# Differential attention: scaling the second map and adding it on GpSimd, with the head norm's epsilon scaled to match

## The reference, cut to what matters

```python
a = softmax(s1) - lam * softmax(s2)          # s1, s2: scores with ALiBi bias and chunk mask
o = a @ v                                    # per head, 128 wide
o = rms(o, g_sub) * (1 - lambda_init)        # o / sqrt(mean(o^2) + EPS), EPS = 1e-6
```

## Time before, and its profile

| what | us |
|---|---|
| three runs: median (lowest, highest) | 3034.1 (3030.89, 3037.03) |
| the profiled execution, span from its first to its last instruction | 3033.2 |
| PE busy in the span | 2847.4 (94%) |
| DVE busy | 1369.0 (45%) |
| ACT busy | 967.3 (32%) |
| POOL busy | 494.7 (16%) |
| stage of differential attention, about | 547 to 943 |
| stage of latent attention, about | 943 to 1354 |
| `mix_out`, about | 1354 to 1600 |
| `mlp`, about | 1600 to 3033 |

### The profile page before, as it was taken

One profiled execution on the slowest core, in us unless ns is written; L12 is line 12 of the kernel. 1 busy time (PEld: TensorE's weight loads), 2 busy tenths in 40 slices (PEclk: granted clock), 3 DMA queues, 4 the chain that ended last, 5 costly groups with the idle time before them and its releaser, 6 DMA issues. The chain is left out here.

```text
span 3033.2 us, 35888 instructions
## 1 busy us (share of the span) xinstructions
PE 2847.4 (94%) x12859; PEld 2275.7 (75%) x12859; DVE 1369.0 (45%) x2743; ACT 967.3 (32%) x1561; POOL 494.7 (16%) x321
## 2 busy tenths in 40 slices
PE   6998898699996999989979999999999999999997
PEld 5996686566674777757767888888887888888886
DVE  5113303688892554534434344343436434343444
ACT  5112212467673443435542121211123111111212
POOL 0010001122220212110012111111114111111112
PEclk8999998799997999999999999999999999999999
DMA  5323218933413111114452111111126111111112
GB/s 181 120 102 94 80 49 290 222 77 88 112 42 126 57 56 60 46 49 130 141 180 91 56 42 55 41 51 46 42 97 222 56 42 48 49 41 55 41 49 97
DMA packets 229877, 267.27 MB, mean 88 GB/s; under 512 B 19392, under 2 KB 174416, under 8 KB 227456
## 3 DMA queue, kind: packets, MB, share of 16 engines
q1 hardware_dynamic: 229760, 265.79, 28.8%
HBM read 187.85 MB, written 77.89 MB: 88 GB/s over the span
## 5 line engine op out<-in xcount | busy, mean ns | idle before, releaser
L1890 DVE TENSOR_TENSOR ff_acc<-ff_acc,ff_ps 128x1024 f32<-128x1024 f32 x240 | 292.3, 1218 | 718.5 <-PE ff_ps L1964 718.5
L1947 PE MATMUL ff_ps<-ff_u_hi,ff_w_hi 128*128 128x512 f32 x1024 | 406.4, 397 | 12.5 <-DVE ff_w_lo L1878 12.5
L1947 PE MATMUL ff_ps<-ff_u_lo,ff_w_hi 128*128 128x512 f32 x1024 | 406.1, 397 | 0.0
L1947 PE MATMUL ff_ps<-ff_u_hi,ff_w_lo 128*128 128x512 f32 x1024 | 405.9, 396 | 0.0
L1964 PE MATMUL ff_ps<-ff_w_hi,ff_hid_hi 128*128 128x512 f32 x1024 | 399.3, 390 | 1.6 <-DVE ff_acc L1890 1.5
L1964 PE MATMUL ff_ps<-ff_w_lo,ff_hid_hi 128*128 128x512 f32 x1024 | 399.1, 390 | 0.0
L1964 PE MATMUL ff_ps<-ff_w_hi,ff_hid_lo 128*128 128x512 f32 x1024 | 398.4, 389 | 0.0
L1855 ACT ACTIVATE work<-ff_ps 128x1024 f32<-128x1024 f32 x64 | 65.6, 1025 | 738.5 <-PE ff_ps L1947 738.5
L1819 POOL TENSOR_TENSOR work<-work 128x1024 f32<-128x1024 f32 x64 | 121.2, 1894 | 1081.9 <-ACT work L1855 1081.9
L1364 PE MATMUL da_ps_s<-da_keys,da_qs 128*128 128x420 f32 (+17 forms) x704 | 219.8, 421 | 33.3 <-DMA late_ident<-in_ident 15.7
L1947 PEld LDWEIGHTS ff_ps<-ff_u_hi,ff_w_hi 128*128 128x128 f32 x1024 | 193.0, 188 | 59.3 <-DVE ff_w_lo L1878 12.9
(11 more groups left out here) (179 smaller groups left out, 4859.3 us busy)
## 6 DMA issues: line engine op xcount, KB each, us to landing
ff_w_raw<-in_w_ff SPq DMA_DIRECT2D x64, 512.0 KB, 4.2
work<-in_w_ff SPq DMA_DIRECT2D x64, 512.0 KB, 3.5
ni_xt<-in_x SPq DMA_DIRECT2D x16, 512.0 KB, 4.3
mo_y<-scr_yT SPq DMA_DIRECT2D x16, 512.0 KB, 5.7
work<-in_x SPq DMA_DIRECT2D x16, 512.0 KB, 4.9
scr_h<-mo_h SPq DMA_DIRECT2D x16, 512.0 KB, 3.3
ff_h_in<-scr_h SPq DMA_DIRECT2D x16, 512.0 KB, 4.3
out<-ff_acc SPq DMA_DIRECT2D x16, 512.0 KB, 5.2
```

The lines of the kernel that those rows point to most:

```text
L1890: dve.tensor_tensor(acc[:, t], acc[:, t], ps2[t % 2][:, :], ALU.add).then_inc(part_added, 1)
L1947: m = pe.matmul(ps1[e][:, cols], w[:, e, k], a[:, k, cols], start=k == 0 and i == 0, stop=k == KD - 1 and i == 2)
```

## The change

For the differential attention only:

- The first map stays unnormalised. Its row sums go into a tile `total1` that keeps all 64 of them (4 heads x 16 rows).
- The step `scale` now stands after the second component and the step `end` is gone. In `scale`, DVE makes the reciprocal of the second sum and the ratio (minus lambda) x t1 / t2; then GpSimd scales the second map in place by the ratio and adds it onto the first, in two instructions with a wait between them.
- DVE waits, before it writes a new row into `second`, for GpSimd's addition of the row two before.
- The list of steps changes with this: the planner's cost of `end` is gone, and a group's first turn stands behind the `scale` of its last row.
- At the end of the stage the 64 sums are squared and multiplied by EPS on ACT, transposed on PE, copied on DVE and stored to DRAM; SP waits for the store.
- In `mix_out` each tile loads the scaled epsilons, spread over the 128 partitions, into `y_rstd` (128x512, one more transfer of 256 KB for a tile); DVE adds the mean from PSUM onto them, and Ln works on the sum instead of on PSUM with a constant bias.

```diff
-                        if c == 0:
+                        if c == COMPS - 1:
                             later.append((SCALE_AFTER, ("scale", 0, i)))
-                        if c == COMPS - 1:
-                            later.append((END_AFTER, ("end", 0, i)))
...
-            return META + P * (step[2] + 1) + 250 if step[0] == "end" and da else 0
+            return 0
...
-                                e[0] == "end" and e[2] - NT * e[1] == 4 * g + 3 - NT * back for e in rows_part[at + 1:]):
+                                e[0] == "scale" and e[2] - NT * e[1] == 4 * g + 3 - NT * back for e in rows_part[at + 1:]):
...
+                if da:
+                    sp.wait_ge(total_copied, 1)
+                    sp.dma_start(scr.eps_total, eps_rows[:, :]).then_inc(total_stored, 16)
+                    sp.wait_ge(total_stored, 16)
...
                 def scaled(h, i, u, **at):
-                    hold(pool, inv_ready, NT * h + i + 1)
-                    pool.tensor_scalar(row(i, u), row(i, u), inv[:, i % 2, 0:1], 1.0, ALU.mult,
-                                       ALU.mult).then_inc(first_scaled if da else probs_ready, 1)
+                    if da:
+                        second_row = comp_row(i, 1, u)
+                        hold(pool, ratio_ready, NT * h + i + 1)
+                        pool.tensor_scalar(second_row, second_row, ratio[:, i % 2:i % 2 + 1], 1.0, ALU.mult,
+                                           ALU.mult).then_inc(second_scaled, 1)
+                        hold(pool, second_scaled, NT * h + i + 1)
+                        pool.tensor_tensor(row(i, u), row(i, u), second_row, ALU.add).then_inc(probs_ready, 1)
...
+                    sums = total1[:, ds(NT * h + i, 1)] if da and c == 0 else total[:, i % 2, c:c + 1]
                     act.activation(comp_row(i, c, u), comp_row(i, c, u), ACT.Exp, bias=nmax[:, i % 2, c:c + 1], scale=scale,
-                                   accum_out=total[:, i % 2, c:c + 1]).then_inc(exp_ready, 1)
+                                   accum_out=sums).then_inc(exp_ready, 1)
...
+                if da:
+                    act.wait_ge(ratio_ready, NT * H)
+                    act.activation(total1[:, :], total1[:, :], ACT.Square, scale=math.sqrt(EPS)).then_inc(total_squared, 1)
...
+                    if da and c == 1 and k0 == 0 and not (isinstance(h, int) and h == 0 and i < 2):
+                        dve.wait_ge(probs_ready, NT * h + i - 1)
...
                 def invert(h, i, u, **at):
+                    if da:
...
+                        dve.wait_ge(exp_ready, NT * COMPS * h + COMPS * (i + 1))
+                        dve.reciprocal(inv[:, i % 2, 1:2], total[:, i % 2, 1:2]).then_inc(inv_ready, 1)
...
+                        dve.tensor_scalar(ratio[:, i % 2:i % 2 + 1], inv[:, i % 2, 1:2], lam[:, 3:4], total1[:, ds(NT * h + i, 1)],
+                                          ALU.mult, ALU.mult).then_inc(ratio_ready, 1)
+                        return
...
-                def end(h, i, u, **at):
...
-                    dve.reciprocal(inv[:, i % 2, 1:2], total[:, i % 2, 1:2]).then_inc(inv2_step, 1)
...
-                    dve.tensor_scalar(inv2[:, i % 2:i % 2 + 1], inv[:, i % 2, 1:2], lam[:, 3:4], None, ALU.mult).then_inc(inv2_step, 1)
...
-                    dve.scalar_tensor_tensor(out=row(i, u), in0=comp_row(i, 1, u), scalar=inv2[:, i % 2:i % 2 + 1], in1=row(i, u),
-                                             op0=ALU.mult, op1=ALU.add).then_inc(probs_ready, 1)
...
+                if da:
+                    dve.wait_ge(total_turned, 1)
+                    dve.tensor_copy(eps_rows[:, :], ps_t[0][0:DA_H * NT, 0:P]).then_inc(total_copied, 1)
...
+                if da:
+                    pe.wait_ge(total_squared, 1)
+                    pe.transpose(ps_t[0][0:DA_H * NT, 0:P], total1[:, :], ident[:, :]).then_inc(total_turned, 1)
...
                     sp.dma_start(y[:, u], scr.yT[:, :, ds(t * P, P)].rearrange("f p t -> p f t")).then_inc(y_loaded[u], 16)
+                    of_tile = scr.eps_total.rearrange("(h t) p -> t h p", h=DA_H)[ds(t, 1)]
+                    sp.dma_start(y_rstd[:, u], of_tile.broadcast_to([P, DA_H, P])).then_inc(y_loaded[u], 16)
...
-                        act.wait_ge(y_loaded[u], 16 * nth + 16)
+                        act.wait_ge(y_loaded[u], 32 * nth + 32)
...
-                        act.wait_ge(mean_ready, s + 1)
-                        act.activation(y_rstd[:, :], ps_r[:, :], ACT.Ln, bias=eps[:, :]).then_inc(y_log_ready, 1)
+                        act.wait_ge(y_eps_added, s + 1)
+                        act.activation(y_rstd[:, u], y_rstd[:, u], ACT.Ln).then_inc(y_log_ready, 1)
...
+                        dve.wait_ge(mean_ready, s + 1)
+                        dve.wait_ge(y_loaded[u], 32 * nth + 32)
+                        dve.tensor_tensor(y_rstd[:, u], ps_r[:, :].rearrange("p (f t) -> p f t", f=DA_H), y_rstd[:, u],
+                                          ALU.add).then_inc(y_eps_added, 1)
```

More of the change, by code:

```diff
@@ L850, in attention @@
         inv = mem.sb(f"{name}_inv", [P, 2, COMPS])
-        inv2 = mem.sb(f"{name}_inv2", [P, 2])
+        ratio = mem.sb(f"{name}_ratio", [P, 2])
+        total1 = mem.sb(f"{name}_total1", [P, DA_H * NT]) if da else None
+        eps_rows = mem.sb(f"{name}_eps_rows", [DA_H * NT, P]) if da else None
         lam_in = mem.sb(f"{name}_lam_in", [P, 4, DA_HD])
@@ L991, in attention @@
         PHASES = (((0, 1), ((1, 3),), 0.2, 7), ((2,), ((0, 0), (0, 1)), 0.15, 7), ((3,), ((0, 2),), 0.2, 7))
-        SCALE_AFTER, END_AFTER = (2, 5) if da else (2, 2)
+        SCALE_AFTER = 2
         STEPS = head_steps()
@@ L1169, in scaled @@
                 def scaled(h, i, u, **at):
[L1171 to L1173 removed]
+                    if da:
[5 more added lines that the diff above has]
+                        pool.tensor_tensor(row(i, u), row(i, u), second_row, ALU.add).then_inc(probs_ready, 1)
+                    else:
+                        hold(pool, inv_ready, NT * h + i + 1)
+                        pool.tensor_scalar(row(i, u), row(i, u), inv[:, i % 2, 0:1], 1.0, ALU.mult,
+                                           ALU.mult).then_inc(probs_ready, 1)
                 heads(pool, {"scale": scaled})
@@ L1329, in _ @@
                     split_q(0, 0)
-                heads(dve, {"chunk": chunk, "scale": invert, "end": end, "turn": copy, **splits(split_q, split_keys)})
+                heads(dve, {"chunk": chunk, "scale": invert, "turn": copy, **splits(split_q, split_keys)})
+                if da:
+                    dve.wait_ge(total_turned, 1)
+                    dve.tensor_copy(eps_rows[:, :], ps_t[0][0:DA_H * NT, 0:P]).then_inc(total_copied, 1)
             @block.tensor
@@ L1440, in mix_out @@
         x_loaded = [mem.sem(f"mo_x_loaded{u}") for u in range(2)]
-        sq_ready, mean_ready, y_log_ready, y_rstd_ready, y_normed = (mem.sem(f"mo_y_{s}") for s in ("sq", "mean", "log", "rstd", "normed"))
+        sq_ready, mean_ready, y_eps_added, y_log_ready, y_rstd_ready, y_normed = (mem.sem(f"mo_y_{s}") for s in ("sq", "mean", "eps_added", "log", "rstd", "normed"))
         y_hi_ready, y_lo_ready, mix_ready = (mem.sem(f"mo_{s}") for s in ("y_hi_ready", "y_lo_ready", "mix_ready"))
@@ L1997 @@
     "u_hi": (P, KD, SEQ // 2), "u_lo": (P, KD, SEQ // 2),
-    "h": (SEQ, D),
+    "h": (SEQ, D), "eps_total": (DA_H * NT, P),
 }
```

30 lines of the change are left out of this document (13 added, 17 removed).

## The result

The changed kernel takes 3073.8 us (median of 4 runs, 3064.0 to 3078.4) against 3035.6 for the kernel before on the same chip: ratio 1.0123, 95% interval 1.0102 to 1.0144. The forecast was 3053 with a range up to 3072, so the measured time lies above the range. The sign was right; the growth is twice the one forecast (38 us against 18.5).

A forecast was written before the change was run, and what follows sets the result against it. DVE was taken as the attention stage's bound, PE close behind. Terms -2.4 + 11.8 + 0.9 + 4.3 + 1.2 + 2.7 = +18.5 us on a 3033.2 span gave 3051.7, said as 3053; 8-in-10 range 3035 to 3072.

The forecast's parts named there:

- The addition: GpSimd in the attention stage: about 2.1 ns a column, 4.5 us for the widest row, no collision with DVE.
- The border: Between heads: PE turns 9.4 us after row 15's last maximum, pausing 4.7 us instead of 1.6; DVE stands too.
- Without any of these the head would take 90.0 - 10.9 = 79.1 us.: Head 2: without the 10.9 us its weight loads wait, PE needs 79.1 us, all the change can win.
- waits of 8.5 less: Head 3: 8.5 us of waits saved, set against border and group-2 turn costs; 85.1 us instead of 87.2 before a fall.
- Clock, 5 x 3 us: Heads 1 to 3: five new pauses of about 5 us each cost a clock fall of 3 us, 15 us together.
- all five pauses named: Two pauses each in heads 1 and 2 (border, row 12's q), one in head 3; about 5 us each.
- q of group 3: Heads 1 and 2: q, queued behind delayed keys leaving at T + 29.0, makes row 12 wait some 5 us.
- End of the stage: Attention's end: last turn +4.3 us, squares, transpose, copy and store of the sums +1.2 us.
- two more issues and a longer landing: Start of `mix_out`, ahead of the first square, plus an extra hop in the first two steps: +2.7 us (0 to 5).
- the rivals: Whole kernel: clock holds, 3038 (0.20); faster, 3026 (0.12); GpSimd becomes the bound, 3073 (0.13); nothing moves, no separate chance.
- that rival's 3073: Attention: GpSimd becomes the bound if additions cost above about 2.8 ns a column; +38 us, 3073; chance 0.13.
- three signs of being wrong: Attention: keys leave no later, clock stays at 1.00, or the addition costs something else than 2.1 ns a column.

The follow-up runs named there:

- the old weight: Changed kernel with the planner's list again counting a row's `scale` as its width + 250, as `end` did, GpSimd still adding; ratio 1.0129 to the kernel before.
- the filled pause: Changed kernel with five extra 128x512 matmuls on PE before its wait for the first turn of group 3; ratio 1.0133 to the kernel before.
- the run with q moved in the kernel before: Kernel before the change, with q of group 3 issued ahead of the next head's keys and bias in SP's list; 3023.2 us, ratio 0.9973.

## Where the prediction was right, and the steps that failed

- **The addition** (4.5 us for the widest, 2.1 ns a column): right, 4.53. No collision with DVE: its pass over the scores has a median of 586 ns for both maps, 587 and 580 before. The Trainium skill's "SBUF — State Buffer", section "Who interferes with whom", says that a DVE instruction with at most one input in SBUF, outside the two-port modes, does not contend with GpSimd; these traces agree. DVE's busy time fell by 19.0 us in head 2, not by the 23 of the prediction (78.9 to 56).
- **The border** (turn at T + 9.4, pause 4.7, DVE idle 5 us): right, 9.7, 5.0 and 5.5.
- **"Without any of these the head would take 90.0 - 10.9 = 79.1 us."** This is the step that failed. I took the waits of PE's weight loads for PE's; of 10.9 us PE itself waited 5.1, and without them the head is 84.8 us long, not 79.1. The run without the addition measured what all of DVE's relief and a chain as short as before bring: 2.9 us in head 2. In head 3 I had counted "waits of 8.5 less" to offset the border, but PE itself waited there for only 2.9 us before. That is 5.6 of the 6 us missing there. The rest is a new wait of 1.3 us for ACT's copy and a fall of 1.6 between rows 7 and 11, against a fall at the border that cost 0.3 instead of 3. Heads 1 and 2 came out near the forecast (+13.5 against +11.8) by luck: two errors met, less was given back, and the clock cost less. (The 90.04 and 87.2 us of the prediction are cut 0.24 us behind T; from T to T they are 89.85 and 87.47. Nothing hangs on it.)
- **The order of the list** was worked out for the border, not for rows 8 to 11. There it costs 1.4 us a head, and 1.6 more when the clock falls (shown by the old weight). This term was missing; taking the old order back did not pay by itself, since the border grew.
- **Clock, 5 x 3 us**: it fell behind all five pauses named and once more in head 3. But the falls at the border cost 1.1, 0.9 and 0.3 us here (shown by the filled pause) and those at row 12 some 1.7 each, together 5.7 and not 15. The sixth cost 1.6. The prediction's "by the rows three in four" is also not what its rows show: of 3.23, 3.34 and 2.98 us two brought a fall. The Trainium skill's "TensorE: Matmul & The Clock Gate", section "HAM oscillation", tells of PE going back to half rate at each wait for data between bursts of matmuls; the trace agrees for the pauses of 4.8 us (15 of 15 heads). Shorter ones are not settled by length: the waits of 2.2 and 3.5 us at row 12 brought a fall here, and one of 2.2 us in head 2 before the change did not.
- **q of group 3**: late and waited for (3.5 us in head 2), as forecast, but not in every execution, and in its place stands a wait of 1.7 us for row 11's addition. The keys left at T + 32.3, not T + 29.0, since little of the border's delay was given back. In head 0 PE waited for q for 3.1 us before and waits 5.6 now, and there are new waits of 1.7 us for row 11's addition, 1.2 for ACT's copy and 1.5 more for the bias, against 5.0 less for DVE's banks. So the head did not become 2.4 us shorter but 1.7 longer.
- **End of the stage**: +3.8 against +5.5.
- **`mix_out`**, "two more issues and a longer landing": +11.3 against +2.7. This is the term of the sum that was most mis-sized. I priced the replicated load like the 512 KB load beside it. Two mechanisms, both shown: a replicated source (12.0 us to land instead of 6.1, which makes 7.8 us at the first product), and DVE's wait for the gain, which was harmless as long as DVE's first work came late and now stood ahead of the new addition (5.1 us by moving it). The two overlap: the gain lands late because it is queued behind the replicated loads. With both removed the first product came at 12.0 us. The step time of `mix_out` did stay.
- Of the rivals none took place. GpSimd did not become the bound: at 59.8 us of 97 it was idle over a third of the time. The measured time reached that rival's 3073 by other roads. Of the three signs of being wrong none showed either: the keys left later, the clock fell, and the addition costs 2.1 ns a column. The errors lay in terms that had no sign of their own.

What stays open is why the same pause lets the clock fall in one execution and not in another (at the last turn: 2.8 us in two profiles; between rows 7 and 11: 1.3 us, in some heads and not in others). The extra 5 us of the run with q moved in the kernel before are the same question.

## What to carry to other kernels

When an engine with slack is relieved, read what the bound engine's own instructions waited for, not what its prefetches waited for; only the first can be won. Moving work to a slower engine costs its length wherever that work is the last step before a hand-over: give such rows to the fast engine and the rest to the slow one. When a new instruction is put at the head of a stage, look at every wait and transfer that stood ahead of it unnoticed, and load a value that all partitions share once.

## What the runs showed of the hardware

- A load that gives 128 partitions the same four pieces of 512 bytes took 12.0 us for 256 KB, the same load from different pieces 6.1, and the load queued behind it 13.9 against 6.4. A broadcast of 4 KB rows (the gain, 512 KB) showed nothing of that: 5.8 to 7.0 us.
- GpSimd's addition of two tensors took 4.53 us for 2064 columns and 0.49 for 144, with DVE's passes over the scores (one input in PSUM) beside it. DVE's longest pass stayed at 662 ns (664 before), and the four additions of 2064 columns lie within 3 ns of one another.
- What a fall of the clock costs depends on what PE has to do in its stretch. It was 1.6 us between rows 7 and 11, where nothing hid it; 0.1 to 1.1 (once 3.0) at the border, where part of the stretch lay in the pause; and 5.0 at the end of a stage in which PE works alone, by two executions with the same pause of 2.8 us.
- Pauses of PE of 4.8 us brought a fall each time (15 of 15 heads), pauses of 1.3 us between rows 7 and 11 in 9 of these 15 heads.
